# Head-sum products over the whole array, and decay and rate logits as stacked fp32r products, in a three-branch block on one core

## The reference, cut to what matters

```python
h = rmsnorm(x, norm_w)                       # 256 tokens x 2048
p = h @ w_in                                 # 2048 x 17,552 columns
pa, pb, pc, pg = split(p)                    # RWKV7, Mamba2 (SSD), short convolution, gates

# branch a (RWKV7), 16 heads of 64 channels
pa = p_a + mu * (previous token's p_a - p_a)
r, k, v, g, dw, da = split(pa)               # dw, da: 64 columns each
log_w = -softplus(-(w0 + tanh(dw) @ w2)) - 0.5
decay = exp(-exp(log_w))
a     = sigmoid(a0 + da @ a2)                # w2, a2: 64 x 1024
kk    = k * k_k;  k = k * (1 + (a - 1) * k_a)
kh    = kk / max(sqrt(sum over the head of kk*kk), 1e-12)
S     = S * decay - (S kh) (kh*a)^T + v k^T  # per head and token;  y = S r
var   = mean over the head of (y - mean)^2
yn    = (y - mean) * rsqrt(var + 64e-5) * ln_w + ln_b
oa    = (yn + sum(r*k*r_k) * v) * silu(g)
# branches b and c, then
merged = sum over branches of sigmoid(p_gate) * (o @ w_branch)
out    = rmsnorm(x + merged @ w_out, final_norm_w)
```

## Time and profile before

| | |
|---|---|
| time, 3 runs | 1115.96 us median (1115.70 to 1116.47) |
| profiled execution | 1117.01 us, of which the recorded span is 1115.3 us |
| granted TensorE clock | 0.996 of full speed over the span |
| PE, DVE, ACT, POOL busy | 99%, 72%, 55%, 4% of the span |
| prelude | 0 to 101 us |
| eight visits | 101 to 640 us, 68 us each, the last one with gate chunks |
| gates and outputs | 640 to 1115 us |

### The profile page before, as it was taken

The page is one execution under the profiler, slowest core; times in us unless marked ns, Lnnn a source line. Parts: engine busy times, 40 slices in busy tenths (PEclk is TensorE's granted clock), DMA queues, the critical chain, the costliest instruction groups (busy, mean ns, idle before and its releaser), DMA issues.

```text
span 1115.3 us, 22920 instructions
## 1 busy us (share of the span) xinstructions
PE 1100.5 (99%) x8006; PEld 918.8 (82%) x8006; DVE 807.8 (72%) x1257; ACT 610.7 (55%) x934; POOL 42.5 (4%) x68
## 2 busy tenths in 40 slices
PE   7999999999999999999999999999999999999997
PEld 5888888888888888888888888888888888888885
DVE  6888889798897988889888858445555555556564
ACT  6666575665756657576475645445344544435443
POOL 2000000000000000000000120000000000000000
PEclk8999999999999999999999999999999999999999
DMA  7766656556475655656556565666666576667663
GB/s 200 206 162 181 171 141 171 157 160 167 129 189 148 180 152 141 183 144 176 143 164 176 153 189 156 222 207 189 191 191 196 158 226 200 195 179 270 212 192 109
DMA packets 254556, 197.24 MB, mean 177 GB/s; under 512 B 23111, under 2 KB 206640, under 8 KB 254128
## 3 DMA queue, kind: packets, MB, share of 16 engines
q1 hardware_dynamic: 251748, 195.81, 60.6%
q10 hardware_dynamic: 2764, 0.85, 0.3%
HBM read 193.71 MB, written 2.11 MB: 176 GB/s over the span
## 4 chain that ended last, share of the span: by engine, by line
PE 98%; DVE 1%; ACT 1%; ACTq 0%; issue 0%
PE ps L1372 31%; PE ps L1375 15%; PE ps L1473 12%; PE ps L1475 12%; PE ps L1474 12%; PE ps L1761 3%; PE ps L1762 3%; PE ps L1760 3%; PE ps L1507 1%; PE ps L1685 1%; PE ps L1546 0%; PE ps L1402 0%; PE ps L1645 0%; PE ps L1709 0%; PE ps L1554 0%; PE ps L1582 0%
## 5 line engine op out<-in xcount | busy, mean ns | idle before, releaser
L853 DVE TENSOR_TENSOR wlo<-raw,whi 128x1024 fp32r<-128x1024 f32 x352 | 434.3, 1247 | 218.4 <-ACT whi L455 216.6
L1372 PE MATMUL ps<-hx,whi 128*128 128x512 f32 x1424 | 516.2, 405 | 1.4 <-DVE hx L884 1.3
L455 ACT ACTIVATE whi<-raw 128x1024 fp32r<-128x1024 f32 (+1 forms) x356 | 370.3, 1051 | 252.8 <-PE ps L1475 182.4
L1375 PE MATMUL ps<-hx,wlo 128*128 128x256 f32 x1424 | 399.6, 281 | 0.0
L1372 PEld LDWEIGHTS ps<-hx,whi 128*128 128x128 f32 x1424 | 268.0, 188 | 69.1 <-issue 6.9
L1375 PEld LDWEIGHTS ps<-hx,wlo 128*128 128x128 f32 x1424 | 269.8, 189 | 1.1 <-DVE lots L893 0.5
L1473 PE MATMUL ps<-whi,hx 128*128 128x512 f32 x384 | 150.4, 392 | 0.0
L1475 PE MATMUL ps<-whi,hx 128*128 128x512 f32 x384 | 149.6, 390 | 0.0
L1474 PE MATMUL ps<-wlo,hx 128*128 128x512 f32 x384 | 149.5, 389 | 0.0
L1475 PEld LDWEIGHTS ps<-whi,hx 128*128 128x128 f32 x384 | 72.1, 188 | 15.0
L1473 PEld LDWEIGHTS ps<-whi,hx 128*128 128x128 f32 x384 | 72.1, 188 | 14.9 <-issue 0.2
(11 more groups left out here) (285 smaller groups left out, 1048.4 us busy)
## 6 DMA issues: line engine op xcount, KB each, us to landing
raw<-in_w_in SPq DMA_DIRECT2D x548, 256.0 KB, 3.2
raw<-in_w_branch SPq DMA_DIRECT2D x96, 256.0 KB, 3.7
raw<-in_w_out SPq DMA_DIRECT2D x64, 256.0 KB, 3.7
o<-in_x SPq DMA_DIRECT2D x4, 512.0 KB, 5.6
o<-in_x SPq DMA_DIRECT2D x2, 1024.0 KB, 8.7
acb<-acs_rows SPq DMA_DIRECT2D x7, 256.0 KB, 3.4
out_y<-lots SPq DMA_DIRECT2D x5, 256.0 KB, 2.5
lots<-in_final_norm_w SPq DMA_DIRECT2D x1, 1024.0 KB, 11.5
```

Source lines behind the costliest of these rows:

```text
L455: sc.activation(whi[:, slot, :, 0:width], raw[:, slot, :, 0:width], ACT.Copy).then_inc(hi_done, 1)
L853: tt(wlo[:, slot, :, :], raw[:, slot, :, :], whi[:, slot, :, :].bitcast(F32), ALU.subtract).then_inc(lo_done, 1)
L1372: mm(ps[:, bank, :], whi[:, slot, k, wcol], hx[:, kt].rearrange("p a t -> p (a t)"), start=first, stop=False, skip_group_check=True)
L1375: return mm(ps[:, bank, 0:T], wlo[:, slot, k, wcol], hhi[:, kt, :], start=False, stop=last, skip_group_check=True)
```

## The change

1. The variance and the key norm each become one plain fp32 product over the whole array (`head1` as 128 x 128 weights, 256 columns). The key norm goes behind the logits, the variance behind the products of branch b. ACT's three roots and DVE's three floors become one each.
2. The logits: `lorat` now holds `w2` twice (partitions 0 to 63 and 64 to 127) and `a2` twice. ACT rounds it to `lorah` (t = 13), and POOL subtracts to get `loral`. The rank activations `tanh(dw)` and `da` are stacked as high part and low part over 128 partitions (`lrs`), once in the prelude. Each logit is then two fp32r products of 128 rows and 256 columns.
3. `load_lora` issues four DMAs in place of two, and SP issues them behind the first two strips of the visit, ahead of the chunk and the wait for `ad_ok` that precede L296.
4. Some semaphores are shared (`row_rt`, `row_rs`, `dt_e`).

```diff
             def load_lora(j):
-                sp.dma_start(lorat[0:64, 0, :], rw_w2[0, :, bass.ds(j * P, P)]).then_inc(lora_in, 16)
-                sp.dma_start(lorat[64:128, 1, :], rw_a2[0, :, bass.ds(j * P, P)]).then_inc(lora_in, 16)
+                for w, src in enumerate((rw_w2, rw_a2)):
+                    for h in range(2):
+                        sp.dma_start(lorat[side(h), w, :], src[0, :, bass.ds(j * P, P)]).then_inc(lora_in, 16)
...
                 strip(c + 4, (SC0 + j * P, SC0 + W + j * P))
+                if not last:
+                    sp.wait_ge(s["lora_mm"], j + 1)
+                    load_lora(j + 1)
                 cols = (SC0 + 2 * W + j * P, SC0 + 3 * W + j * P)
...
                     strip(c + 12, cols, quarters=range(1, 4))
-                    sp.wait_ge(s["lora_mm"], j + 1)
-                    load_lora(j + 1)
                     sp.wait_ge(s["seg_ok"], j + 1)
...
+            def lora_split_lo(j):
+
+                pool.wait_ge(s["lora_hi"], j + 1)
+                gp.tensor_tensor(loral[:], lorat[:], lorah[:].bitcast(F32), ALU.subtract).then_inc(s["lora_lo"], 1)
...
                 gp.tensor_tensor(bv, kh, sga[:, 1, :], ALU.mult).then_inc(s["bv_ok"], 1)
+                if not last:
+                    lora_split_lo(j + 1)
...
+            def lora_split_hi(j):
+
+                act.wait_ge(lora_in, j * 64 + 64)
+                sc.activation(lorah[:], lorat[:], ACT.Copy).then_inc(s["lora_hi"], 1)
...
+                    if t == 13 and not last:
+                        lora_split_hi(j + 1)
...
-                        sc.activation(nrm[:, 0:P], C[:, 0:P], ACT.Sqrt, scale=1.0 / 64, bias=eps3[:, 1:2])
-                        for e in range(2):
-                            op = sc.activation(nrm[side(e), P:T], B[side(1 - e), P:T], ACT.Sqrt, scale=1.0 / 64,
-                                               bias=eps3[side(e), 1:2])
-                        op.then_inc(s["var_rt"], 1)
+                        sc.activation(nrm, C[:, 0:T], ACT.Sqrt, scale=1.0 / 64, bias=eps3[:, 1:2]).then_inc(s["var_rt"], 1)
...
-                ts(ksq[:, 0:P], B[:, 0:P], 1e-24, None, ALU.max)
-                for e in range(2):
-                    op = ts(ksq[side(e), P:T], ps[side(1 - e), bank, T:T + P], 1e-24, None, ALU.max)
-                op.then_inc(s["kk_max"], 1)
+                ts(ksq, B[:, 0:T], 1e-24, None, ALU.max).then_inc(s["kk_max"], 1)
...
+                    dve.wait_ge(s["lr_ok"], 2)
+                    for w in range(2):
+                        op = tt(lrs[side(1 - w), w, :], lshift[side(w), :], lrs[side(w), w, :].bitcast(F32), ALU.subtract)
+                    op.then_inc(s["lr_lo"], 1)
...
-            def norm_and_logits(j, bank):
-
-
-                for h in range(2):
-                    for e in range(2):
-                        op = mm(ps[side(e ^ h), bank if h else 5, h * T:h * T + P], head1[side(e), side(e)],
-                                ksq[side(e), h * P:h * P + P], start=True, stop=True)
-                op.then_inc(s["kk_mm"], 1)
-                pe.wait_ge(lora_in, j * 32 + 32)
-                mm(A[:, 0:T], lorat[0:64, 0, :], lr[0:64, :], start=True, stop=True)
-                mm(C[:, 0:T], lorat[64:128, 1, :], lr[64:128, :], start=True, stop=True).then_inc(s["lora_mm"], 1)
+            def norm_and_logits(j):
+
+                pe.wait_ge(s["lora_lo"], j + 1)
+                for w, dst in enumerate((A[:, 0:T], C[:, 0:T])):
+                    mm(dst, lorah[:, w, :], lrs[:, w, :], start=True, stop=False)
+                    op = mm(dst, loral[:, w, :], lrs[:, w, :], start=False, stop=True)
+                op.then_inc(s["lora_mm"], 1)
+                mm(B[:, 0:T], head1[:], ksq, start=True, stop=True).then_inc(s["kk_mm"], 1)
...
-                        for h in range(2):
-                            for e in range(2):
-                                op = mm(ps[side(e ^ h), 6 - h, h * P:h * P + P], head1[side(e), side(e)],
-                                        ysq[side(e), h * P:h * P + P], start=True, stop=True)
-                        op.then_inc(s["var_mm"], 1)
...
+                        mm(C[:, 0:T], head1[:], ysq, start=True, stop=True).then_inc(s["var_mm"], 1)
```

More of the change, by code:

```diff
@@ L167, in build_program @@
         lorat = sb("lorat", [P, 2, P])
-        lr = sb("lr", [P, T])
+        lorah, loral = (sb(n, [P, 2, P], F32R) for n in ("lorah", "loral"))
+        lrs = sb("lrs", [P, 2, T], F32R)
         rowst = sb("rowst", [P, 24])
@@ L232, in build_program @@
             acs_st acb_in seg_ok seg_e seg_g yb_mm ob_d ob_ok sq_ok gn_mm gn_rt gn_r gn_ok osp_hi osp_lo gy_ok
-            mg_ok mt m_hi m_lo out_mm out_ok f_sq f_act f_rs f_ok f_hi stored"""
+            mg_ok mt m_hi m_lo out_mm out_ok f_sq   f_ok f_hi stored"""
         s = {n: sem(n) for n in names.split()}
@@ L408, in main @@
                     kk_unit(j + 1)
+            lora_split_lo(0)
             pool.wait_ge(s["sc_mm"], NG)
@@ L510, in _ @@
                 if c == 6:
+                    lora_split_hi(0)
                     act.dma_start(dsk[:], ssd_d.broadcast_to([P, 2 * CT])).then_inc(dsk_in, 16)
@@ L559, in _ @@
                     act.wait_ge(s["ranks_sh"], 1)
-                    sc.activation(lr[0:64, :], lshift[0:64, :], ACT.Tanh)
-                    sc.activation(lr[64:128, :], lshift[64:128, :], ACT.Copy).then_inc(s["lr_ok"], 1)
+                    sc.activation(lshift[0:64, :], lshift[0:64, :], ACT.Tanh).then_inc(s["lr_ok"], 1)
+                    act.wait_ge(s["lr_ok"], 1)
+                    for w in range(2):
+                        op = sc.activation(lrs[side(w), w, :], lshift[side(w), :], ACT.Copy)
+                    op.then_inc(s["lr_ok"], 1)
                     act.wait_ge(s["dt_v"], 1)
                     sc.activation(dts[:, 2, :], dts[:, 1, :], ACT.Exp, scale=-1.0).then_inc(s["dt_e"], 1)
-                    sc.activation(dtc[:, 2:3], dtc[:, 1:2], ACT.Exp).then_inc(s["dt_ae"], 1)
+                    sc.activation(dtc[:, 2:3], dtc[:, 1:2], ACT.Exp).then_inc(s["dt_e"], 1)
                     act.wait_ge(s["dt_v"], 2)
@@ L798, in row_root @@
                 sc.activation(rowst[:, 2 + b:3 + b], rowst[:, b:b + 1], ACT.Sqrt, scale=1.0 / D, bias=eps3[:, 0:1]
-                              ).then_inc(s["f_act"], 1)
-                act.wait_ge(s["f_rs"], b + 1)
+                              ).then_inc(s["row_rt"], 1)
+                act.wait_ge(s["row_rs"], b + 3)
             row_root(0)
@@ L825, in token_scale @@
             def token_scale(b):
-                dve.wait_ge(s["x_rt"], b + 1)
-                v.reciprocal(rowst[:, 4 + b:5 + b], rowst[:, 2 + b:3 + b]).then_inc(s["x_rs"], 1)
-                dve.wait_ge(s["x_rs"], b + 1)
+                dve.wait_ge(s["row_rt"], b + 1)
+                v.reciprocal(rowst[:, 4 + b:5 + b], rowst[:, 2 + b:3 + b]).then_inc(s["row_rs"], 1)
+                dve.wait_ge(s["row_rs"], b + 1)
                 for at, w in ((0, 2 * P), (2 * P, 4 * P), (6 * P, 10 * P)):
@@ L919, in _ @@
                     dve.wait_ge(s["lora_mm"], 1)
-                    kk_floor(0, 6)
+                    kk_floor(0)
                     kk_recip(0)
@@ L976, in _ @@
                     dve.wait_ge(s["dt_v"], 7)
-                    dve.wait_ge(s["dt_ae"], 1)
+                    dve.wait_ge(s["dt_e"], 2)
                     ts(dts[:, 3, :], dts[:, 5, :], dtc[:, 2:3], -1.0, ALU.mult, ALU.mult).then_inc(s["dt_v"], 1)
@@ L1223, in main @@
                         shift(j + 1, 0)
-                        kk_floor(j + 1, 7)
+                        kk_floor(j + 1)
                     if t == 34:
@@ L1307, in row_scale @@
                     v.tensor_reduce(rowst[:, b:b + 1], rowst[:, 8 + 4 * b:12 + 4 * b], AX.X, ALU.add).then_inc(s["f_sum"], 1)
-                    dve.wait_ge(s["f_act"], b + 1)
-                    v.reciprocal(rowst[:, 4 + b:5 + b], rowst[:, 2 + b:3 + b]).then_inc(s["f_rs"], 1)
-                    dve.wait_ge(s["f_rs"], b + 1)
+                    dve.wait_ge(s["row_rt"], b + 3)
+                    v.reciprocal(rowst[:, 4 + b:5 + b], rowst[:, 2 + b:3 + b]).then_inc(s["row_rs"], 1)
+                    dve.wait_ge(s["row_rs"], b + 3)
                 def scaled(b, q):
@@ L1443, in _ @@
                     op.then_inc(s["dt_tr"], 1)
-                    pe.wait_ge(s["lr_ok"], 1)
+                    pe.wait_ge(s["lr_lo"], 1)
                     pe.wait_ge(s["const_o"], 2)
                     pe.wait_ge(s["kk_sq"], 1)
-                    norm_and_logits(0, 6)
+                    norm_and_logits(0)
             def gate_half(n, i, y, b, first=False):
@@ L1570, in main @@
                     if t == 33 and not last:
-                        norm_and_logits(j + 1, 7)
+                        norm_and_logits(j + 1)
                     if t == 4:
@@ L1695, in main @@
                     if t == V_VAR:
-                        if last:
-                            pe.wait_ge(s["ysq_ok"], j + 1)
```

(8 more changed lines are left out.)

8 lines of the change are left out of this document (4 added, 4 removed).

## The result

The kernel after takes 1119.02 us (median of 12 runs, 1118.13 to 1120.14), the kernel before 1115.88 in the same sessions (12 runs, 1115.08 to 1116.47). The ratio is 1.0027, 95% interval 1.0020 to 1.0035: slower by 3.1 us. The profiled execution of after took 1119.46 (span 1117.7, clock 0.995), that of before 1117.01.

A forecast was written before the change was run, and what follows sets the result against it. TensorE (PE) was taken as the bound, busy 342.00 of 342 us. PE's stream -2.8 us plus stops of +5.8 from late loads and POOL's product gave +3.0: median 1119.0 us, range 1113.0 to 1123.5.

The forecast's parts named there:

- PE's gain: PE's own instruction stream, with its stops at t = 4 gone: 2.8 us shorter in all, 1113.2 if nothing came late.
- the stops: PE waiting at t = 18 or 19: 1.0 us in visits 1, 3, 5, 0.53 in 2, 4, 6, 1.2 for visit 0; together 5.8.
- t = 33: PE's step with logits and key norm: 1.23 to 1.26 us in place of 1.55, so 0.30 less.
- t = 28: PE's step with branch b and the variance: 1.68 us, up to 0.1 more, against 1.73; -0.2 us in all.
- The prelude's step: The prelude's run of the step that is at t = 33 in the visits: a gain of 0.2 us.
- SP: SP's four moved loads ahead of L296: 2.6 us of issue less the gaps, so L296 comes 1.65 us later.
- The landing: Score blocks there 1.65 us behind their last issue, as with the inverses, leaving DVE 0.83 us to spare before its solve.
- POOL: `lora_split_lo` at t = 13, amid DVE's solve: delays DVE 0.4 us per visit, bounds 0 and 0.73.
- room enough: Rival: score blocks land early or SP issues faster, POOL's product costs nothing, PE keeps its 2.8: 1113.2 us; chance 0.20.
- half of it: Rival: the room covers SP's delay and only POOL's 0.4 comes through, 0.9 us of stops: 1114.1 us; chance 0.12.
- No room at all: Rival: blocks land just when DVE asks and the port lock costs the full 0.73; 14 us of stops, 1127 us; chance 0.10.
- Dearer products: Rival: the four fp32r products take 0.2 us each, +2.5 us: 1121.5 with the forecast's stops, 1115.7 with room enough; chance 0.08.

The follow-up runs named there:

- experiment 1: Changed kernel with the four loads, ACT's rounding and POOL's subtraction moved back late, PE's new products kept: 1110.39 us, ratio 0.9956 to the kernel before.
- experiment 3: Changed kernel with ACT's rounding and POOL's subtraction moved back late, the four loads still early: 1116.00 us, ratio 1.0004 to the kernel before.
- experiment 4: Kernel before with four loads of the rank weights in place of two, moved ahead of the chunk and the score blocks: 1120.66 us, ratio 1.0047.
- experiment 5: Kernel before with its two loads moved ahead of the chunk and the score blocks: 1116.06 us, ratio 1.0004.
- experiment 2: Changed kernel with the four loads directly behind the four DMAs of `ad`, POOL's product still at t = 13: 1112.98 us, ratio 0.9981 to the kernel before.

## Why the prediction was right, and where it only came out right

The time, the sign and the mechanism were as predicted. The sum was not as good as it looks: two of its terms, PE's gain and the stops, were too small by about as much on opposite sides, and that they cancelled was luck.

**Steps of PE.** t = 33: 1.26, predicted 1.23 to 1.26. t = 28: 1.78, predicted 1.68 to 1.78, so the first whole product behind the tiles did pay for the change: from L1724 to the next L1391 (154.82) are 0.35, where the same product at t = 33 (L1419) takes 0.24. The three stops at t = 4 fell away. The prelude's step was to gain 0.2 and lost 0.15: the profile shows a wait of 0.20 for ACT's square of the keys (L503) ahead of the first logit. ACT makes it at 93.88 in place of 92.81, since DVE's two new subtractions (0.85) stand ahead of the keys. The prediction had them delay only the way to t = 4, for 0.2. There too PE stops, ahead of the scores of visit 0: one pair takes 0.69 in place of 0.35. The 35 pairs before it, slow before and fast now, give 0.2 of that back. Seven steps at t = 33, eight at t = 28, the prelude and the stops at t = 4 make -7 x 0.29 + 8 x 0.04 + 0.15 - 0.3 = -1.9, against the -2.8 of the prediction.

**The pitch** was not in the prediction at all. In after every stretch in the visits is fast; in before the 19 pairs behind t = 28 and the 43 behind t = 33 are slow or partly slow, and in visits 2, 4 and 6 also the 56 pairs between the scores and t = 18. The 19 pairs are 0.12 shorter in after. The 43 pairs are 0.31 shorter in visits 1, 3, 5 and 6, where they were slow throughout, and 0.20 in visits 0, 2 and 4. The 56 pairs are 0.37 shorter in three visits. That is 7 x 0.12 + 4 x 0.31 + 3 x 0.20 + 3 x 0.37 = 3.8 us in seven visits. So PE alone gained not 2.8 but 5.3 (experiment 1, by the medians; 1.9 + 3.8 makes 5.7, and experiment 1 has one slow stretch of 56 pairs left, 0.37). Whether the new products cause the fast pitch is not shown, since what sets it is open; it is fast in the visits of every kernel here that has them, but for one stretch each in experiments 1 and 3. That is the term that was mis-sized on the fast side; the rows for it were in the trace, in the plainest part of the stream, where I had read no distances.

**SP.** Predicted 1.65 late, measured 1.93 in visits 1 to 6: the four loads take 181.39 - 178.67 = 2.7, not 2.6, and the gaps gave 0.8, not 0.95. In visit 0 it is 2.8, since the four take 3.50 there, and the last of them alone 1.35 in place of 0.55; experiment 4 shows the same. In experiment 5, with two loads, the long issue in visit 0 is the second half of the chunk behind them (1.29 in place of 0.37). The landing, which the prediction took from the inverses as 1.65 behind the end of the last issue, is 1.23: the four L301 end at 182.38 + 2.77 = 185.15, and DVE starts at 186.38. Wherever DVE waits for the blocks in experiments 3 to 5, it is 1.2 to 1.3 too. So DVE had 183.78 - 181.30 - 1.23 = 1.25 to spare, not 0.83, and its delay is 1.93 - 1.25 = 0.68, predicted 0.82. The one error makes up for the other in part.

**POOL.** 0.38, predicted 0.4. It falls on one product of the solve with two inputs, which takes 0.75 in place of 0.33. By the exclusive lock of which the Trainium skill speaks ("SBUF — State Buffer", section "SBUF: two separate sides") the one that starts second blocks until the first is done. The trace agrees that DVE's product is held up while POOL's keeps its 0.74, but it shows a smaller loss: from the start of DVE's product (190.06) to the end of POOL's (190.62) are 0.56, and DVE lost 0.42.

**The stops.** Odd visits: predicted 1.0, measured 0.96. By the prediction's own way of counting it would be 0.68 + 0.38 - 0.23 = 0.83; the room of 0.23 was worth only 0.1 (experiments 2 and 3), since PE starts L1394 0.06 behind the end of L1122 and the step behind it then takes 0.1 longer. So here too errors cancelled. Even visits: predicted 0.53, measured 0.96 as well. Their extra room of 0.31 was no property of these visits; it was the slow pitch of the 56 pairs between the scores and t = 18, which makes PE ask later, by 0.37. With the pitch the room went. Experiment 4 bears this out: its slow 56 pairs stand in visits 1 and 4, and there PE has no stop at t = 18, while visits 2, 3, 5 and 6 have one; all six last 68.7 to 68.8. Visit 0: predicted 1.2, of which 0.2 ahead of the scores; behind them it is 69.55 - 67.39 = 2.16, mostly from SP's 2.8. Together 6 x 0.96 + 2.16 = 7.9, predicted 5.8.

So the predicted -2.8 + 5.8 = +3.0 was measured as -5.3 + 7.9 = +2.6, where the medians of before and after differ by 3.1. Of the signs that it named, SP's delay (1.5 to 1.7) and the step at t = 28 (1.7) came out somewhat larger, and PE's idle time in visits 1 to 6 (0.5 to 1.2) is 0.40 and 0.07, since a part of each stop shows as a longer distance and not as idle time (0.57 and 0.24 by distance). Of the rivals, "room enough" and "half of it" fell with the DMA wait in the list. "No room at all" fell with experiment 5. "Dearer products" fell with t = 33: L1416 and L1417 follow each other at 0.12.

## What to carry to other kernels

Where an engine issues DMAs in order, a load that is not urgent goes behind the transfers that somebody waits for; here four small loads put ahead of them, and one GpSimd product put beside VectorE's chain, cost 8 us and ate a gain of 5, of which some 4 came from a change of pitch that nobody had planned. Before a stop is priced, look whether the room differs from one repetition to the next, and why: room that another inefficiency makes goes when that goes. And read the distances in the stream that does not change, not only in the steps that do.

## What was not expected of the hardware

- A pair of fp32r products (512 and 256 columns) has two pitches at the same granted clock, 0.3467 and 0.3533 us, each mostly kept over a whole stretch of 19 to 151 pairs. The slow one is a cycle of three pairs of which two are 0.01 longer. It is worth some 4 us here, and what chooses it is open.
- A whole-array fp32 product of only 16 columns between fp32r products costs 0.2 us.
- Four loads of 64 partitions take SP 2.7 us in visit 1 and 3.5 in visit 0, where the second pair takes 1.99 in place of 1.19. Why is open.
- The four transfers of `ad` are there 1.23 us behind the end of their last issue, the two of the inverses only 1.65 behind theirs.
